# Selection transfers in pieces over nine rounds, and two RWKV turns in each round of the tail

## The reference, cut to what matters

```
x += 0.5 * SwiGLU_a(rms(x))
h = rms(x); p = h @ W_in
x += W_out [ RWKV7(p_rw) | mLSTM(p_ml) | NSA(p_nsa) ]
x += MemXAttn(rms(x), mem)
x += 0.5 * SwiGLU_b(rms(x))
```

## Time and profile before

| | us |
|---|---|
| median of 3 runs | 3886.96 |
| lowest and highest | 3881.82 and 3899.01 |
| the profiled execution's own time | 3879.58 |
| its span, first to last instruction | 3877.8 |
| PE busy in the span | 3564.3 (92%) |
| DVE busy | 1297.1 (33%) |
| ACT busy | 566.7 (15%) |
| POOL busy | 180.4 (5%) |
| the tail, in the trace | 1776 to 2268 |

### The profile page before, as it was taken

One profiled execution on the slowest core, in us unless ns is written; L12 is line 12 of the kernel. 1 busy time (PEld: TensorE's weight loads), 2 busy tenths in 40 slices (PEclk: granted clock), 3 DMA queues, 4 the chain that ended last, 5 costly groups with the idle time before them and its releaser, 6 DMA issues. The chain is left out here.

```text
span 3877.8 us, 44326 instructions
## 1 busy us (share of the span) xinstructions
PE 3564.3 (92%) x18084; PEld 2309.5 (60%) x18084; DVE 1297.1 (33%) x3074; ACT 566.7 (15%) x1261; POOL 180.4 (5%) x282
## 2 busy tenths in 40 slices
PE   7999889999999999996977868968799999999998
PEld 4666566666567777675655544434466556656776
DVE  3445503223313223315534467722432122111111
ACT  1000001000011101002213336610110001000000
POOL 3111100000000000000010100000000000000000
PEclk8999999999999999997778879989999999999999
DMA  6565554232334332335345320050042333233443
GB/s 158 178 183 176 168 143 114 82 105 65 92 111 115 100 96 74 103 114 101 61 80 188 117 84 9 6 171 17 1 130 76 103 109 87 77 99 103 127 129 94
DMA packets 607237, 401.76 MB, mean 104 GB/s; under 512 B 90636, under 2 KB 584060, under 8 KB 602556
## 3 DMA queue, kind: packets, MB, share of 16 engines
q1 hardware_dynamic: 578956, 314.10, 29.7%
q0 software_dynamic: 13824, 67.12, 5.5%
q10 hardware_dynamic: 14256, 17.71, 1.3%
HBM read 367.95 MB, written 36.13 MB: 104 GB/s over the span
## 5 line engine op out<-in xcount | busy, mean ns | idle before, releaser
L400 PE MATMUL psum<-arena 128*128 128x384 f32 (+1 forms) x4224 | 1336.4, 474 | 24.6 <-DVE arena L535 15.9
L400 PEld LDWEIGHTS psum<-arena 128*128 128x128 f32 x4224 | 799.3, 192 | 492.4 <-issue 31.3
L410 PE MATMUL psum<-arena 128*128 128x384 f32 (+1 forms) x2112 | 660.8, 472 | 0.0
L410 PEld LDWEIGHTS psum<-arena 128*128 128x128 f32 x2112 | 399.3, 191 | 234.7 <-issue 3.7
L433 PE MATMUL psum<-arena 128*128 128x384 f32 (+3 forms) x816 | 270.5, 488 | 0.0
L549 DVE SCALAR_TENSOR_TENSOR arena<-arena,psum 128x384 f32<-128x384 f32 (+1 forms) x132 | 70.3, 532 | 580.9 <-ACT arena L487 580.8
L487 ACT ACTIVATE arena<-psum 128x384 f32<-128x384 f32 (+1 forms) x132 | 62.4, 472 | 1354.0 <-PE psum L400 1354.0
L565 DVE SCALAR_TENSOR_TENSOR arena<-psum,arena 128x384 f32<-128x384 f32 (+1 forms) x96 | 51.4, 536 | 505.1 <-PE psum L410 505.1
L558 DVE TENSOR_TENSOR arena<-psum,arena 128x384 f32<-128x384 f32 (+1 forms) x132 | 70.7, 536 | 424.1 <-PE psum L400 423.2
L433 PEld LDWEIGHTS psum<-arena 128*128 128x128 f32 (+1 forms) x816 | 153.0, 192 | 95.9 <-issue 18.9
L442 PE MATMUL psum<-arena 128*128 128x264 f32 (+3 forms) x576 | 136.6, 399 | 0.0
(11 more groups left out here) (557 smaller groups left out, 3272.2 us busy)
## 6 DMA issues: line engine op xcount, KB each, us to landing
arena<-in_ffa_up SPq DMA_DIRECT2D x132, 512.0 KB, 5.3
arena<-in_ffb_up SPq DMA_DIRECT2D x132, 512.0 KB, 5.2
arena<-in_ffa_down SPq DMA_DIRECT2D x48, 704.0 KB, 4.6
arena<-in_ffb_down SPq DMA_DIRECT2D x48, 704.0 KB, 4.5
arena<-in_w_in SPq DMA_DIRECT2D x27, 1024.0 KB, 5.9
arena<-in_w_in SPq DMA_DIRECT2D x9, 1056.0 KB, 5.9
pT<-arena ACTq DMA_DIRECT2D x32, 192.0 KB, 5.1
arena<-xs SPq DMA_DIRECT2D x2, 2176.0 KB, 19.1
```

The source lines that it names most:

```text
L400: ins = mm(b[:, 0:n], w[:, g, k], hC[:, k, 0:n], start=(k == 0), stop=(k == KD - 1))
L410: ins = mm(b[:, 0:n], w[:, k], actT[:, k, 0:n], start=(k == 0), stop=(k == FH - 1))
```

## The change

`NSA_LOADS` goes from 6 to 10, so the selection lane begins in round 36 on PE, DVE and ACT (still in 26 on SP and POOL). On SP the lane yields after the stores of the mLSTM states, `NRW` comes in two transfers and `NR` in four with a yield behind each, and the constants, the first queries and the copy to the output have rounds of their own. In the weave of the tail the RWKV lane stands twice on every engine: first in the round, and again behind the samples' lane and ahead of the selection lane (on SP ahead of `states_sp`). It is one generator, so each round takes two of its turns: turns 2r and 2r + 1 in round r.

```diff
-        NSA_FIRST, NSA_LOADS = 26, 6
+        NSA_FIRST, NSA_LOADS = 26, 10
...
         def nsa_sp(sp):
+            rows = lambda o: o.rearrange("t c g d -> t (c g d)")
             ml_states_out(sp)
+            yield
             ml_over(sp)
-            sp.eng.dma_start(NRW, pR[0:TP, 256:512].rearrange("(i p) c -> p i c", p=P),
-                             allow_slow_non_contiguous=True).then_inc(loads_for_vector, 16)
+            for q in range(2):
+                sp.eng.dma_start(NRW[:, 4 * q:4 * q + 4], pR[4 * q * P:(4 * q + 4) * P, 256:512].rearrange("(i p) c -> p i c", p=P),
+                                 allow_slow_non_contiguous=True).then_inc(loads_for_vector, 16)
+                yield
+            for q in range(4):
+                sp.eng.dma_start(NR[:, 2 * q:2 * q + 2], pR[2 * q * P:(2 * q + 2) * P, 512:1048].rearrange("(i p) c -> p i c", p=P),
+                                 allow_slow_non_contiguous=True).then_inc(loads_for_vector, 16)
+                yield
             for g in range(2):
                 sp.eng.dma_start(wpr[64 * g:64 * g + 64], I["nsa_wpos"][0].rearrange("l c g d -> l (c g d)"),
                                  allow_slow_non_contiguous=True).then_inc(pool_weights_in, 16)
-            sp.eng.dma_start(NR, pR[0:TP, 512:1048].rearrange("(i p) c -> p i c", p=P),
-                             allow_slow_non_contiguous=True).then_inc(loads_for_vector, 16)
...
+            yield
             sp.wait_ge(gpsimd_for_sync, sp.due(gpsimd_for_sync))
...
-            rows = lambda o: o.rearrange("t c g d -> t (c g d)")
+            yield
             sp.eng.dma_start(rows(O["cmp_p"][0, 0]), pR[0:TP, 256:512],
                              allow_slow_non_contiguous=True).then_inc(outputs_stored, 16)
-            for _ in range(NSA_LOADS + 4):
+            for _ in range(NSA_LOADS + 4 - 9):
                 yield
...
-            v.wait_ge(loads_for_vector, v.due(loads_for_vector, 16 * 5))
+            v.wait_ge(loads_for_vector, v.due(loads_for_vector, 16 * 9))
...
-            for _ in weave(lane(sp, 2, rw_begin_sp, rw_make_sp, rw_chain_sp), lane(sp, 2, ml_begin_sp, ml_make_sp, ml_chain_sp), sa_sp(sp), states_sp(sp), chain(idle(NSA_FIRST), nsa_sp(sp))):
+            rw = lane(sp, 2, rw_begin_sp, rw_make_sp, rw_chain_sp)
+            for _ in weave(rw, lane(sp, 2, ml_begin_sp, ml_make_sp, ml_chain_sp), sa_sp(sp), rw, states_sp(sp), chain(idle(NSA_FIRST), nsa_sp(sp))):
...
-            for _ in weave(lane(pe, 2, rw_begin_pe, rw_make_pe, rw_chain_pe), lane(pe, 2, ml_begin_pe, ml_make_pe, ml_chain_pe), chain(idle(3), sa_pe(pe)), chain(idle(NSA_FIRST + NSA_LOADS), nsa_pe(pe))):
+            rw = lane(pe, 2, rw_begin_pe, rw_make_pe, rw_chain_pe)
+            for _ in weave(rw, lane(pe, 2, ml_begin_pe, ml_make_pe, ml_chain_pe), chain(idle(3), sa_pe(pe)), rw, chain(idle(NSA_FIRST + NSA_LOADS), nsa_pe(pe))):
```

More of the change, by code:

```diff
@@ L4226, in _ @@
                     pass
-            for _ in weave(lane(gp, 2, rw_begin_gp, rw_make_gp, rw_chain_gp), lane(gp, 2, ml_begin_gp, ml_make_gp, ml_chain_gp), chain(idle(3), sa_gp(gp)), chain(idle(NSA_FIRST), nsa_gp(gp))):
+            rw = lane(gp, 2, rw_begin_gp, rw_make_gp, rw_chain_gp)
+            for _ in weave(rw, lane(gp, 2, ml_begin_gp, ml_make_gp, ml_chain_gp), chain(idle(3), sa_gp(gp)), rw, chain(idle(NSA_FIRST), nsa_gp(gp))):
                 pass
@@ L4245, in _ @@
                     pass
-            for _ in weave(lane(act, 2, rw_begin, rw_make_act, rw_chain_act), lane(act, 2, ml_begin_act, ml_make_act, ml_chain_act), chain(idle(3), sa_act(act)), chain(idle(NSA_FIRST + NSA_LOADS), nsa_act(act))):
+            rw = lane(act, 2, rw_begin, rw_make_act, rw_chain_act)
+            for _ in weave(rw, lane(act, 2, ml_begin_act, ml_make_act, ml_chain_act), chain(idle(3), sa_act(act)), rw, chain(idle(NSA_FIRST + NSA_LOADS), nsa_act(act))):
                 pass
@@ L4310, in _ @@
                     pass
-            for _ in weave(lane(v, 2, rw_begin, rw_make_dve, rw_chain_dve), lane(v, 2, ml_begin_dve, ml_make_dve, ml_chain_dve), chain(idle(3), sa_dve(v)), chain(idle(NSA_FIRST + NSA_LOADS), nsa_dve(v))):
+            rw = lane(v, 2, rw_begin, rw_make_dve, rw_chain_dve)
+            for _ in weave(rw, lane(v, 2, ml_begin_dve, ml_make_dve, ml_chain_dve), chain(idle(3), sa_dve(v)), rw, chain(idle(NSA_FIRST + NSA_LOADS), nsa_dve(v))):
                 pass
```

## The result

The changed kernel takes 3925.49 us (median of 4 runs, 3920.91 to 3925.79) against 3887.14 of the kernel before in the same measurement: a ratio of 1.0076, 95% interval 1.0051 to 1.0101. On another chip it was 1.0069 (1.0046 to 1.0092). It is slower, by more than half a per cent, and lies outside the predicted range of 3848 to 3910. Its profiled execution took 3920.9, 41.3 us more than that of before.

The account below looks back on a forecast made before the run. The prediction took the tail to be bound by one turn waiting for another, no engine; -78.9 (late rounds) + 76 (early rounds) + 3 (SP's pieces) = 0.1 us, so 3880 us stated, range 3848 to 3910.

Parts of the forecast that it names:

- Leaves the late rounds: Rounds 28 to 59: RWKV work, its idle and page waits go, some latencies come back; 78.9 us less.
- The pages' 24.2: Late rounds: PE's 24.2 us of waits for pages and windows should go.
- The samples' own latencies: Rounds 28 to 37, samples' lane alone: uncovered waits for ACT's copies, DVE's mask and ACT's exponential; 9 us back.
- The softmax and search at the end: Rounds 52 to 56: selection lane's long DVE turns, with too little PE work beside them; 14 us back (7 to 20).
- The cause of the pages' delay: SP and POOL: mLSTM state stores issue slowly, POOL stands 27.2 us for their landing, next gathers queue behind.
- Comes to the early rounds: Rounds 0 to 27: moved RWKV work and bare waits, less gaps filled; 76 us more.
- the same 62.0 us of PE work: RWKV's PE work leaving rounds 28 to 59, counted at the same 62.0 us in rounds 0 to 27.
- My rival of filled rounds: Rounds 0 to 12: RWKV fills preparation gaps, 40 us instead of 20, and PE's clock rises; 3850, chance 0.27.
- 7 + 27 - 20 = 14: Rounds 0 to 27: 7 us of turn 50's stall, 27 of bare waits between neighbouring turns, less 20 of idle filled.
- The pair from turn 17 to 18: Neighbouring RWKV turns on PE, early rounds: DVE's answer from L1108 to L1126 lies bare, 4.5 us.
- The clue I gave for neighbouring turns: Sign of the slower rival (bare waits 45 us, fill 5; 3913, chance 0.21): L1370, L1304, L1327 wait over 45 us for DVE.
- SP's pieces: SP's queue: split transfers cost nothing themselves, but a remaining burst beside gathers is charged 3 us (0 to 12).

Follow-up runs that it names:

- the delayed kernel: Kernel before plus 42 dummy DVE instructions between its last tail work and the meeting of the engines; 3918.24 us, ratio 1.0059.
- the counter-experiment: Changed kernel with the second RWKV turn moved behind the mLSTM lane and ahead of the samples' lane; 3894.22 us, ratio 1.0005.

## Why the prediction was wrong, point by point

**What bounds it** was read rightly: no engine, but one turn waiting for another. The forecast was a difference of two sums of nearly 80, so that an error of a third in one is the whole result.

**Leaves the late rounds** held: 86 against 75.9. Of the 10 us more, 7 are the clock: the moved work was put at 62.0, and PE's busy part fell by 69.1. The pages' 24.2 went, with POOL free (the row of L3124); L1649 left DVE's softmax and waits 9.1 in place of 14.8. The samples' own latencies were put at 9; L2675 waits 5.2 for its copies and L2693 6.9 for the exponential, 12.1 together where it was 1.9. The softmax and search at the end were put at 14 (7 to 20); L2739 pays 12.2 more. The cause of the pages' delay was half right: the stores hold POOL, as the chain of the earlier trace rows had it, but with seven eighths of them cut POOL still waits 19.5 and the pages stay late by 14.0. What takes the delay away is that RWKV's second turns stand there (with them such waits add to 1.6 us at most in any of the kernels, without them to 14.0 at least).

**Comes to the early rounds** failed: 111 for 76. Two terms were mis-sized.

The first, worth 19 us: *the same 62.0 us of PE work* was priced at the clock of the rounds it left, 0.82. It arrives in rounds at 0.62 to 0.81, and with it those of 13 to 26 fell to 0.72, while the late ones rose to 0.89. The work measured 80.7 there and 69.1 where it left. Over the whole tail that is 11.5 us. That it is the clock shows in the product of busy time and granted clock over the tail, which stays the same: 379.5 at 0.78 is 296, 391.0 at 0.76 is 297. The kernel with the turn moved ahead shows the same 80 busy, so it hangs on the rounds and not on the place. How much of the 11.5 is the change is less sure: the delayed kernel, with the tail's order of before, had 0.76 and 392.2 as well (298), and the medians of six and six profiles are 16 apart. My rival of filled rounds had the clock rising with more work; it stood at 0.65 in the first window, after 0.62.

The second, worth 16: *7 + 27 - 20 = 14* of waits against fill. It was 30.3 in the changed kernel's profile and 11.0 with the turn ahead of the samples. The total of bare waits and fill thus came near for a turn in a good place, though no run measures the 27 and the 20 apart. It missed what the place does: I had asked what stands between neighbouring turns on PE, and not what stands ahead of the turn in DVE's and ACT's lists. The clearest case is L1407, held 8.0 us for a DVE turn behind mLSTM's turn and the samples' top-eight search. The longest wait, 11.5, is none: one of 11.2 to 11.9 stands at that place in the kernel before and with the turn ahead. The pair from turn 17 to 18, which I had priced at 4.5, came with 5.8 (L1304), and with the samples' turn between it was 1.1. The clue I gave for neighbouring turns, L1370, L1304 and L1327 waiting over 45 us for DVE, did not come: 3.2, 5.8 and 4.3 for DVE, and 16.0 for ACT. That rival's time was nearest (3913), its mechanism only in part the one at work.

**SP's pieces** were put at 3 (0 to 12): nothing that can be told from 0, by the ratio of 0.9987. The later start of the lane, which I had only seen as the softmax's term, costs 0.4% without second turns (1.003 against 0.9987); in the changed kernel it can't be told from none.

**Behind the tail** I had counted nothing. The changed kernel's profile lost 16.9 us there, 12 of them in a half-clock stretch that two profiles of the kernel before with small edits have too, and that the changed one is rid of in its second profile. The other 5 are inside the 10 us by which the profiles without the stretch differ behind the tail. And the sum was set on one profiled execution of 3879.6, which is at the lower end of what the kernel before shows (medians of 3892 to 3898 on five more measurements); the range should have had that as well.

**The range** reached to 3910 by the bounds of the waits alone. With the clock's 11.5 as a term it would have reached 3922, still under the 3925 of the first measurement and just above the 3921 of the second.

## What to carry to other kernels

When a turn is moved between rounds, read for each engine what stands ahead of it in that engine's list, not only what follows it on the bound one: a multiplication of 0.4 us behind another lane's search cost PE 8.0 us on one side of that lane and 1.2 at most on the other. And look for the same wait in the kernel before and in the counter-experiment before calling it the cost of the change: the longest one here, 11.5 us, stood in all three. One profile isn't enough for a difference of ten us either: tails with the same order of work lay 13 us and more apart. Price moved TensorE work at the granted clock of the rounds it goes to, and expect these rounds' clock to move as well. Where a forecast is a small difference of large terms, test the order of lanes first: the place of one lane was worth 0.7%, which was the whole loss.

## What the runs showed of the hardware

TensorE stood at half clock for 34.1 us in one place of some executions and not of others: in four profiles of seventeen (the changed kernel, the delayed one, the one with the turn ahead and the start at 32, and the one before with both stores cut), each time at 2.93 us for four matmuls of 128x384 in place of 1.56. From the first to the last matmul of that line it is 658.4 us in each of the four, and 646.4 to 648.3 in the others. The last of the four took 3886.7 in that run against a median of 3877.6.

One matmul stood 3.4 to 15.9 us with nothing to wait for but its own issue, in the six profiles whose second turn stands behind the samples from round 0 on; with the turn ahead of them from round 0 on its longest was 1.1 and 1.5, and in the nine others there was none. It was still there, with 3.4 and 8.9 us, when seven eighths of the small stores beside it were left out.
